# Gates projected last and channel-major, with the last retention items and three output-stage tiles beside these products

## The reference, cut to what matters

```python
p = modulate(x, sh1, sc1) @ w_in[l]          # columns: q, k, v, gate g, conv a, conv b, 512 each
q = apply_rope(split_heads(p[..., Q_OFF:K_OFF], RET_DK), cos, sin)
k = apply_rope(split_heads(p[..., K_OFF:V_OFF], RET_DK), cos, sin) * (RET_DK ** -0.5)
o_f, _ = retention_scan(q, k, v, lg_f, s_f)
o_b, _ = retention_scan(flip_seq(q), flip_seq(k), flip_seq(v), lg_b, s_b)
# retention_readout: per-head normalisation of o, then
on = on * gn_w + gn_b
ret = jax.nn.silu(g) * on
# conformer_conv: u = a * sigmoid(b); depthwise conv of 31 taps; silu(layer_norm(u))
mix = jnp.concatenate([ret, conv], axis=-1) @ w_out
x = layer_norm(ALPHA * x + g1 * mix, ln1_w, ln1_b)
x = mlp_sublayer(x, ...)                     # squared ReLU, 4096 wide, then a second layer norm
```

## Time and profile before

| | us |
|---|---|
| median of three runs (2905.45 to 2911.14) | 2907.34 |
| the profiled execution, its own time | 2907.55 |
| its span, first to last instruction | 2905.7 |
| PE busy | 2726.5 (94%) |
| DVE busy | 1966.5 (68%) |
| POOL busy | 1083.0 (37%) |
| ACT busy | 719.2 (25%) |

### The profile page before, as it was taken

The page is one execution under the profiler, slowest core; times in us unless marked ns, Lnnn a source line. Parts: engine busy times, 40 slices in busy tenths (PEclk is TensorE's granted clock), DMA queues, the critical chain, the costliest instruction groups (busy, mean ns, idle before and its releaser), DMA issues.

```text
span 2905.7 us, 38116 instructions
## 1 busy us (share of the span) xinstructions
PE 2726.5 (94%) x13644; PEld 2242.3 (77%) x13644; DVE 1966.5 (68%) x3283; ACT 719.2 (25%) x1490; POOL 1083.0 (37%) x1081
## 2 busy tenths in 40 slices
PE   6999999797999999999999699998888999999996
PEld 4778878576888888888888478888677888888885
DVE  4699983856776677677668889873765454454456
ACT  3233334534111111111111323334433111111111
POOL 1344454754111111111112645564762323323325
PEclk9999999798999999999999899999899999999998
DMA  8322322621222222222220222212521111111111
GB/s 244 94 85 76 101 75 82 181 76 45 66 72 70 81 72 72 72 72 73 73 38 29 83 66 61 62 50 58 159 73 44 51 43 51 51 43 51 51 43 66
DMA packets 246658, 214.69 MB, mean 74 GB/s; under 512 B 60384, under 2 KB 203280, under 8 KB 246544
## 3 DMA queue, kind: packets, MB, share of 16 engines
q1 hardware_dynamic: 149488, 120.94, 13.9%
q10 hardware_dynamic: 97056, 92.29, 10.4%
HBM read 190.56 MB, written 22.63 MB: 73 GB/s over the span
## 4 chain that ended last, share of the span: by engine, by line
PE 82%; DVE 8%; POOL 4%; DMA 2%; issue 1%; ACT 1%; SPq 1%; POOLq 0%; ACTq 0%; DVEq 0%
PE bank L624 15%; PE bank L626 15%; PE bank L625 15%; PE bank L1146 9%; PE bank L1147 9%; PE bank L1148 9%; PE bank L708 1%; PE bank L1008 1%; PE bank L1079 1%; PE bank L1009 1%; PE bank L1010 1%; PE bank L1053 1%; DVE x_hl L1620 1%; PE bank L1078 1%; PE bank L1064 1%
## 5 line engine op out<-in xcount | busy, mean ns | idle before, releaser
L1583 POOL TENSOR_TENSOR w_lo<-raw,w_hi 128x1024 fp32r<-128x1024 f32 x120 | 288.4, 2404 | 1124.8 <-ACT w_hi L1414 1124.8
L1850 DVE TENSOR_TENSOR work<-work 128x512 f32<-128x512 f32 (+1 forms) x160 | 158.0, 987 | 472.1 <-ACT work L1402 471.2
L1146 PE MATMUL bank<-x_hl,w_hi 128*128 128x512 f32 (+1 forms) x1280 | 475.4, 371 | 0.0
L1147 PE MATMUL bank<-x_hl,w_hi 128*128 128x512 f32 (+1 forms) x1280 | 473.2, 370 | 0.0
L1148 PE MATMUL bank<-x_hl,w_lo 128*128 128x512 f32 (+1 forms) x1280 | 472.9, 369 | 0.0
L1874 DVE TENSOR_TENSOR work<-work,bank 128x512 f32<-128x512 f32 x576 | 390.1, 686 | 122.3 <-PE bank L626 111.4
L624 PE MATMUL bank<-w_hi,h_hi 128*128 128x512 f32 x1152 | 451.1, 392 | 7.3 <-DVE work L1874 5.4
L625 PE MATMUL bank<-w_lo,h_hi 128*128 128x512 f32 x1152 | 449.5, 390 | 0.0
L626 PE MATMUL bank<-w_hi,h_lo 128*128 128x512 f32 x1152 | 449.3, 390 | 0.0
L1755 DVE SCALAR_TENSOR_TENSOR bank<-work,bank 128x512 f32<-128x512 f32 (+1 forms) x580 | 406.9, 702 | 17.8
L1414 ACT ACTIVATE w_hi<-raw 128x1024 fp32r<-128x1024 f32 x120 | 126.8, 1059 | 775.6 <-PE bank L626 583.9
(11 more groups left out here) (141 smaller groups left out, 4575.1 us busy)
## 6 DMA issues: line engine op xcount, KB each, us to landing
raw<-in_w_ff ACTq DMA_DIRECT2D x128, 512.0 KB
work<-in_w_ada SPq DMA_DIRECT2D x48, 512.0 KB
plain_words<-in_w_ada ACTq DMA_DIRECT2D x64, 256.0 KB
raw<-in_w_in SPq DMA_DIRECT2D x60, 256.0 KB
plain_words<-in_w_ada SPq DMA_DIRECT2D x16, 512.0 KB, 12.6
raw<-in_w_out SPq DMA_DIRECT2D x10, 512.0 KB
gate_rows<-work SPq DMA_DIRECT2D x72, 64.0 KB, 1.6
retention_rows<-work SPq DMA_DIRECT2D x72, 64.0 KB, 1.6
```

The lines of the kernel that those rows point to most:

```text
L1146: nc.tensor.matmul(o, slot(mlp_slot(l, f), 0)[:, wc], x_hi[:, k, cols], start=k == 0, stop=False)
L1147: nc.tensor.matmul(o, slot(mlp_slot(l, f), 0)[:, wc], x_lo[:, k, cols], start=False, stop=False)
L1583: nc.gpsimd.tensor_tensor(slot(mlp_slot(l, sl), 1), raw[:, un % 2, :], slot(mlp_slot(l, sl), 0).bitcast(F32), ALU.subtract).then_inc(w_rea ...
L1850: nc.vector.tensor_tensor(a32, a32, a32, ALU.mult).then_inc(S["h_sq"], 1)
```

## The change

The gate columns leave the Q groups. Every Q group becomes 3 x 128 columns (`QKV`) for ten tiles, the K/G halves of pair 3 go, and a last group `("G", 0)` is added: four units of 128 gate channels, channel-major. For a run of four tiles each unit is two steps, "G" (the first four of the eight contraction blocks) and "H" (the rest, in the same bank); for the two context tiles of layer 0 it is one step "F". ACT writes silu of the product to `g_out`, and one DMA per unit and run stores it. `IN_UNITS` goes from 24 to 28.

In the output stage the first `EARLY = 3` tiles are worked off inside the plan, beside the last items and the gate steps: loads, statistics, conv transposes, mixed transposes, high and low parts. The loop that remains starts with their products. The gate now meets the retention rows after the transposes: ACT applies gn_w and gn_b per channel, POOL multiplies by the gate and makes the low part of that half; DVE keeps the low part of the conv half. The planner's room for taps becomes 6 x 256 per Q step with queries.

```diff
-IN_UNITS, OUT_UNITS = 24, 8
+IN_UNITS, OUT_UNITS = 28, 8
...
-GROUPS = [("AB", 0), ("AB", 1), ("Q", 0), ("AB", 2), ("Q", 1), ("AB", 3), ("Q", 2), ("Q", 3)]
-IN_HALVES = (3,)
+GROUPS = [("AB", 0), ("AB", 1), ("Q", 0), ("AB", 2), ("Q", 1), ("AB", 3), ("Q", 2), ("Q", 3), ("G", 0)]
...
+EARLY = 3
+QKV = 3 * P
...
-        elif i in IN_HALVES:
-            steps += [("K", i, t) for t in tile_order(i)] + [("G", i, t) for t in item_order(layer, i)]
+        elif kind == "G":
+            for r, (_, nt) in enumerate(chunks_of(layer)):
+                steps += [(part, c, r) for c in range(PAIRS) for part in ("GH" if nt == 4 else "F")]
...
-            room = 7 * 2 * P // (1 if kind == "Q" and t in tiles else 2) if kind in "QKG" else 3 * P * chunks_of(layer)[t][1]
+            room = 6 * 2 * P // (1 if t in tiles else 2) if kind == "Q" else 3 * P * chunks_of(layer)[t][1]
...
+            if not posts:
+                hoisted += [(n + 1, ("cv_load", 0)), (n + 1, ("cv_load", 1))]
+                for j in range(EARLY):
+                    hoisted += [(n + 3 + 2 * j, ("cvt", j)), (n + 4 + 2 * j, ("cnorm", j))]
+                    if j >= 2:
+                        hoisted.append((n + 2 * j, ("cv_load", j)))
...
+        while waiting and (PAIRS - 1, tiles[waiting[0]]) in valued:
+            j = waiting.pop(0)
+            run = next(r for r, (t0, nt) in enumerate(chunks_of(layer)) if t0 <= tiles[j] < t0 + nt)
+            gated = max(i for i, st in enumerate(steps) if st[0] in "FH" and st[2] == run)
+            turn = max(n + 7, gated + 3, turn + 2)
+            hoisted += [(n, ("o_load", j)), (max(n, gated + 1), ("g_load", j)), (n + 3, ("gn_cent", j)), (n + 4, ("gn_var", j)),
+                        (n + 5, ("gn_scale", j)), (turn, ("mixtr", j)), (turn + 1, ("mixlo", j))]
+        hoisted.sort(key=lambda x: x[0])
+        plan += [entry for due, entry in hoisted if due <= n]
...
+                sp.wait_ge(S["comb_done"], s0["comb_done"] + n * PAIRS)
+                for j in range(EARLY, n):
+                    cv_load(j)
+                    o_load(j)
...
+                    for i in range(0 if j == EARLY else j - 2, j - 1):
+                        residual(i)
...
+                for j in range(n):
+                    if EARLY <= j + 1 < n:
+                        turn_mix(j + 1)
+                    if EARLY <= j + 3 < n:
+                        turn_conv(j + 3)
+                    project_mix(j)
...
+                    for k in range(4):
+                        last = nc.scalar.activation(X[:, T[j], k * P:(k + 1) * P], ps_m[0][:, k * P:(k + 1) * P], ACT.Identity,
+                                                    bias=gnc[:, 1, k:k + 1], scale=gnc[:, 0, k:k + 1])
+                    last.then_inc(S["ret_aff"], 1)
...
+                def ret_gate(j):
...
+                    pool.wait_ge(S["ret_aff"], s0["ret_aff"] + j + 1)
+                    pool.wait_ge(S["g_in"][j % 2], s0["g_in"] + 16 * (j // 2 + 1))
+                    nc.gpsimd.tensor_tensor(o, o, g_in[:, j % 2, :, :], ALU.mult).then_inc(S["ret_y"], 1)
+                    pool.wait_ge(S["ret_hi"], s0["ret_hi"] + j + 1)
+                    nc.gpsimd.tensor_tensor(x_lo[:, 0:4, cols], o, x_hi[:, 0:4, cols].bitcast(F32), ALU.subtract).then_inc(S["ret_lo"], 1)
```

More of the change, by code:

```diff
@@ L146, in mix_in_plan @@
     group_end = {last_step(UNIT_OF[g] + (1 if g[0] == "AB" else 3)) for g in GROUPS}
-    plan, evacs, posts, ready = [], list(range(len(steps))), [i for i, st in enumerate(steps) if st[0] in "QKG"], []
+    plan, evacs, posts, ready = [], list(range(len(steps))), [i for i, st in enumerate(steps) if st[0] == "Q"], []
     scored, valued, evac_at, taps = set(), set(), {}, []
-    keyed, asked, scans = set(), set(), [[(p, k) for p in range(PAIRS) for k in range(1, NT)] for _ in range(2)]
+    posted, scans = set(), [[(p, k) for p in range(PAIRS) for k in range(1, NT)] for _ in range(2)]
     items = [(p, t) for p in range(PAIRS) for t in item_order(layer, p)]
@@ L153, in mix_in_plan @@
     finished, stored, pause, consumed, fetches = [], [], 3, False, [5]
+    hoisted, waiting, turn = [], list(range(EARLY)), 0
     def load_units(count):
@@ L165, in freed_early @@
         return since < n or (since == n and in_pair)
-    while n < len(steps) or posts or len(valued) < PAIRS * len(tiles) or pieces or finished or stored:
+    while n < len(steps) or posts or len(valued) < PAIRS * len(tiles) or pieces or finished or stored or hoisted:
         if n < len(steps):
@@ L202, in mix_in_plan @@
             kind, p, t = steps[evacs[0]]
-            if kind in "QK" and p and t in tiles and (p - 1, t) not in valued:
+            if kind == "G":
+                evacs.pop(0)
+                continue
+            if kind == "Q" and p and t in tiles and (p - 1, t) not in valued:
                 break
@@ L212, in mix_in_plan @@
             load_units(behind)
-        short = n < len(steps) and steps[n][0] in "AB" and chunks_of(layer)[steps[n][2]][1] < 4
+        short = n < len(steps) and steps[n][0] != "Q" and chunks_of(layer)[steps[n][2]][1] < 4
         k = 0
@@ L225, in mix_in_plan @@
                 p, j = scans[d][0]
-                if (p, order[j - 1]) not in keyed or p and order[j] in tiles and (p - 1, order[j]) not in valued:
+                if (p, order[j - 1]) not in posted or p and order[j] in tiles and (p - 1, order[j]) not in valued:
                     break
@@ L277, in step_counts @@
         "A": before(lambda kind, i, t: kind == "A"),
-        "rope": before(lambda kind, i, t: kind in "QKG"),
-        "kv": before(lambda kind, i, t: kind in "QK"),
-        "gate": before(lambda kind, i, t: kind == "G" or kind == "Q" and t in tiles),
-        "turned": before(lambda kind, i, t: kind in "QKG" and t in tiles)}
+        "Q": before(lambda kind, i, t: kind == "Q"),
+        "gate": before(lambda kind, i, t: kind in "FH"),
+        "turned": before(lambda kind, i, t: kind == "Q" and t in tiles),
+        "bank": [sum(st[0] != "G" for st in steps[:i]) % PROJ_BANKS for i in range(len(steps))]}
 def shape_constants():
@@ L1381, in _ @@
+                for st in range(EARLY, n + 2):
+                    if st - 2 >= EARLY:
+                        mix_high(st - 2)
+                        ret_high(st - 2)
+                    if st < n:
+                        square(st)
+                    if EARLY <= st - 1 < n:
+                        conv_norm(st - 1)
+                    if st in (EARLY, EARLY + 1):
+                        load(l, IN_UNITS + 4 - EARLY + st)
                 load(l, IN_UNITS + 6)
```

639 lines of the change are left out of this document (325 added, 314 removed).

## The result

The changed kernel takes 2922.1 us (median), the kernel before 2907.3 in the same comparison: ratio 1.0048, 95% interval 1.0036 to 1.006. Forecast were 2861.5 us, range 2845 to 2890. So it is slower by 0.5%, which is small but more than the measurement's uncertainty.

The account below looks back on a forecast made before the run. PE bounds the projection with DVE nearly as busy, then come two half-idle holes. First output halves ending 21.1 and 24.9 us sooner give -46 against 2907.55: 2861.5 us, own range 2850 to 2872, with rivals 2845 to 2890.

Parts of the forecast that it names:

- The last tap: End of DVE's convolution work in the projection: forecast at 432.5 us in layer 0 and 1934.0 in layer 1.
- 78.6, 74.5, 61.5 and 60.5: Forecast us: layer 0 from first gate product to gates' end, then to first output half's end; the same for layer 1.
- 12 items (15.7): Layer 0, PE's work behind the last tap: 12 items at 1.31 us each, 15.7 us in all.
- nothing, or at most one POOL split of 2.4 us per group: Cost of other edits (slots, banks, 768-word units, per-channel constants), said to sit where products cover PE.
- rival D: Output stage: ACT's in-order queue makes one tile's chain and the next's statistics add up; 12.2 per tile, 2924; chance 0.04.
- What is late next is tile 3: Behind the last gate store: tile 3's conv load lands 6.6 us later, PE idles, clock falls; stall 8.5 per layer.
- I take 6.95 per full tile: Output stage's first half: a full tile takes 6.95 us instead of 7.56, with PE at 6.85 hiding the 6.2 chain.
- rival B: Output stage: GpSimd's two operations wait for DVE's, making the retention chain and a tile 7.6; +8, 2870 to 2878; chance 0.13.
- PE runs one turn and one product ahead of DVE (6.1 + 4.15 = 10.3): At the last tap, both layers: PE's lead over DVE, 10.3 us, taken off the gates' end.
- rival A: Up to the gates: DVE holds PE back, both layers lose the 10.3 lead; +22 to +28, 2886; chance 0.14.
- unchanged: Second halves, MLP and end, behind the first output halves: forecast to take as long as before.

Follow-up runs that it names:

- e13: e10 with VectorE's order of e9 (conv_shift and conv_stats ahead of the centring): 2862.5 us, ratio 0.9845 to the kernel before.
- e1: The changed kernel with ScalarE's early-tile work one turn later, behind the next item's s_diag and q_diag: 2900.6 us, ratio 0.9975 to the kernel before.
- e6: e1 with the splits of output weight units 28 and 29 behind the last item and tile 2's gate load behind tile 0's mixing: 2891.3 us.
- e7: The changed kernel with ScalarE's early work one turn later (e1), SyncE's new load order (e5), and output weight units 28 and 29 later (e6): 2874.4 us.
- e5: The changed kernel with SyncE's output-stage loads reordered: conv and retention loads earlier, first two residuals beside gates, tile 2's gate load and modulation loads later: 2906.3 us.
- e10: e7 with the conv columns and retention rows of tile 4 also loaded beside the gate products: 2874.3 us, ratio 0.9887 to the kernel before.
- e9: e5 with VectorE doing conv_shift and conv_stats ahead of the centring in the output stage's loop: 2899.1 us, ratio 0.9976 to the kernel before.
- e2: The changed kernel with SyncE's conv loads issued one tile earlier, the fourth tile's already in the plan: 2915.0 us, ratio 1.0026 to the kernel before.
- e11: e7 with eight of the convolution's 31 taps on an eighth of their columns, result not the reference's: 2856.3 us, ratio 0.983 to the kernel before.

## Why the prediction was wrong, step by step

**Right.** The last tap came at 432.6 for 432.5, and in layer 1, less the 15.1 it starts late, at 1932.6 for 1934.0. A Q turn without item took 4.82, with item 6.13, as summed; gate steps without item 2.72. The output stage lost its hole in both layers, and in e13 the stretches last 76.7, 66.7, 63.6 and 53.5 where the sums said 78.6, 74.5, 61.5 and 60.5.

**The step that failed first: "12 items (15.7)" behind the last tap, at 1.31 each.** The sum took an item from a stretch of the old kernel in which ScalarE had nothing else to do. The change put four operations per early tile into ScalarE's queue ahead of the next s_diag, each waiting for another engine; PE's wait for that s_diag stood in the sum at nothing. Item turns of 512 columns took 5.3 to 7.4 us for 4.03 (in e1, without these waits, 4.1 to 6.1). With the weight splits of the first gate turn (of which the prediction counted only POOL's half, "nothing, or at most one POOL split of 2.4 us per group"), the gates' stretches grew by 18.5 and 14.6. Price: 21.6 (e1) and 9.3 (e6), 30.9 us. The prediction did name this mechanism, as rival D (a serial order in ScalarE's queue), and gave it 0.04: it looked for it in the output stage, where no run shows it, and never went through the gate turns. The order of the entries stood in the plan; going through it queue by queue was done for SyncE's first conv load only.

The Trainium skill, "PSUM — Partial Sum Buffer", Engine vs sequencer instructions, says that the queues of ScalarE, VectorE and GpSimd are strictly first in, first out. The trace agrees: s_diag, ready, starts when the square ahead of it has run (475.52 behind 474.98), and e1 changes nothing but this order.

**Second: "What is late next is tile 3", one stall of 8.5 per layer.** Tile 3's load was late as said (4.20 and 5.31 of wait for 6.6 forecast), but tiles 4, 6 and 8 waited as well, since SyncE's loop has every conv load behind a gate load and a residual of other tiles. Price: e7 against e6, 16.9, which takes in the residuals, retention rows and modulation loads of the same queue, and part of e13's 11.9 (tile 4).

**Third: "I take 6.95 per full tile".** The sum of PE's operations was right (6.78 in the good runs), the wait was rival B's. By B GpSimd's operations make it 7.6; measured 7.86, not as a longer chain of the gated half but as VectorE held up by GpSimd: 1.0 and 0.8 us on two instructions. In the changed kernel itself it is covered by the waits for loads (the subtraction takes 0.69 there) and shows only when these are gone (e5, e10): 7.1 us between e5 and e9. e2's tiles take 7.86 and more too, but there only one subtraction in each layer is long (1.74), the others take 0.69, and VectorE waits for retention rows. The page that the prediction cited, "SBUF — State Buffer" of the Trainium skill, Who interferes with whom, says that a VectorE instruction with two SBUF inputs contends with a GpSimd instruction that reads SBUF, and that the port pair they share is an exclusive lock. The trace agrees: both lengthened ones have two SBUF inputs, and neither ends before GpSimd's does. A VectorE instruction with one SBUF input was lengthened as well: the scaling of the mean (128 x 8) takes 0.64 instead of 0.17 in e9, beside the gate multiply, and L1798, which rival B named, has one input too. Why these are slow no run here shows.

**Fourth: "PE runs one turn and one product ahead of DVE (6.1 + 4.15 = 10.3)".** At the last tap (432.6) PE was at the values product of the next turn, and its first gate product came 8.2 us later; two Q turns with their items and a post are 12.9, so its lead was 4.7. Its lead is cut to less when items start again (5.06 of wait at 390.4), because values wait for probabilities that stand behind that turn's taps. So rival A holds for half of its size: the first gate product at 440.9 for 434.4, and 2 to 3 us in layer 1.

**Sum.** The medians fall by 21.6 (e1), 9.3 (e6), 16.9 (e7) and 11.9 (e13), 59.6 in all, from 2922.1 to 2862.5; the forecast was 2861.5. That it fits to 1 us is partly luck: e13 starts its gates 6.3 late (fourth point) and makes up for it with tile 3 and 4 loaded early, where the forecast allowed a stall of 8.5. The other part of the luck lies behind these stages, which the prediction called unchanged. In e13 the half of layer 0 ends 3.6 us and that of layer 1 2.9 us ahead of the forecast's place (for layer 1 with the 21.1 of layer 0 taken off), but from the one to layer 1's first conv product it takes 1034.1 us (1031.1 before) and from the other to the end 803.8 (799.1). At the start of each second half PE now waits for the low part of a weight unit on GpSimd, here in e13; the kernel before has no such wait:

```profile
590.24 0.65 PE L655 MATMUL bank<-h_hi,x_hl 128*128 128x512 f32 x1 [2.10 <-POOL h_lo L651]
```

It is 1.5 us in the changed kernel, and no run takes it away. It is the term that the sum put at "nothing, or at most one POOL split". The clock over layer 1's second half and the transposes behind it is 0.86 in e13 and 0.91 before; what of that is owed to the wait is not shown.

What the forecast left out is not work but order: rivals D (0.04), B (0.13) and A (0.14), each with its own small chance, came together, and nothing in the chances allowed for that.

e13 takes out the waits of ScalarE's and SyncE's queues; VectorE's ahead of the gates stays, as do in layer 1's gates 2.0 us for GpSimd's rotation and 1.8 for a low part. It is 1.5% faster than the kernel before. The change was sound and its order was not.

## What to carry to other kernels

When work is moved beside other work, write out each engine's queue turn by turn, and ask of every moved operation that waits for another engine or a load: who stands behind it, and does PE need that one at once? Put such an operation behind the short operations on PE's round trip, even a turn late; in layer 0's gates that brought one new wait of 1.4 us (e1). Loads belong ahead of any load or store whose wait ends later, and a wait taken away often uncovers the next one: judge a change by the run in which all of them are gone.

## What the runs showed of the hardware

- A VectorE instruction on one column per partition took 1.05 us instead of 0.15, while GpSimd was in the middle of a 1.29 us operation; one on 512 columns 1.71 instead of 0.69. Where the start is the other way round, GpSimd's multiply is the longer one: 1.64 instead of 1.29 in e7.
- A pipeline over four engines can settle into either of two rhythms with the same instructions, 6.78 and 7.86 us a tile, and stays in it to the end of the stage; loads that come earlier moved it into the slower one (e7 to e10), and so did less work ahead of the gates (e7 to e11); another order on one engine brought it back (e10 to e13).
- Four loads of modulation columns, 4 KB each, held SyncE's queue for 5.30 us, longer than one conv load of 256 KB takes from issue to landing (4.0 in the middle).
- A stop of PE of 1 us cost some 1.6 over the four stretches (changed kernel against e13), since behind many of them the clock was at its lower level (products of 512 columns 0.43 apart instead of 0.23).
